# First layer's shift and scale loaded by halves of the features, with the query's first-half products between the halves

## The reference, cut to what matters

```
def modulation(silu_cond, w_mod_l, b_mod_l):
    m = silu_cond @ w_mod_l + b_mod_l
    return jnp.split(m[:, None, :], 6, axis=-1)      # sh1, sc1, g1, sh2, sc2, g2

def modulate(x, w, shift, scale):
    return rms_norm(x, w) * (1 + scale) + shift

sh1, sc1, g1, sh2, sc2, g2 = modulation(silu_cond, lw['w_mod'], lw['b_mod'])
out, ctx_tensors = token_mixer(modulate(x, lw['norm1'], sh1, sc1), lw, rope, ctx)
# in token_mixer: a_q, a_k, a_v, h_q, ... = split(h @ lw['w_in'])
```

## Time and profile before

| | us |
|---|---|
| median of 3 runs | 1380.81 (1379.59 to 1381.5) |
| profiled execution | 1384.76 |
| its span, first to last instruction | 1382.9 |
| PE busy in it | 1292.7 (93%) |
| DVE, ACT, POOL busy | 484.3, 315.1, 271.0 |
| mean granted clock of TensorE | 0.995 |

### The profile page before, as it was taken

How to read it: one execution, slowest core, us unless ns; L and a number is a source line. 1 busy time by engine, 2 the same in 40 slices (tenths; PEclk the granted TensorE clock), 3 DMA queues, 4 the chain that set the end, 5 groups by cost and what they waited for, 6 DMA issues and landing times.

```text
span 1382.9 us, 17520 instructions
## 1 busy us (share of the span) xinstructions
PE 1292.7 (93%) x6873; PEld 732.2 (53%) x6874; DVE 484.3 (35%) x896; ACT 315.1 (23%) x487; POOL 271.0 (20%) x231
## 2 busy tenths in 40 slices
PE   6999999999999898789999999999999998999877
PEld 2665545567555554345546554556755454555433
DVE  1324425865125401011144343388612541101112
ACT  2116624641001100000021563366100110000000
POOL 1640006841010100000028000486111010000001
PEclk9899999999999999999999999999999999999999
DMA  9799425762633999999984113377355299899997
GB/s 359 247 312 338 154 93 184 246 243 82 242 148 140 367 425 422 424 424 426 419 314 156 65 63 120 123 246 258 114 204 205 80 358 422 334 424 426 425 427 294
DMA packets 114586, 371.88 MB, mean 269 GB/s; under 512 B 17601, under 2 KB 32609, under 8 KB 97873
## 3 DMA queue, kind: packets, MB, share of 16 engines
q1 hardware_dynamic: 84320, 329.70, 61.2%
q0 software_dynamic: 6608, 21.96, 4.4%
q10 hardware_dynamic: 23584, 19.21, 4.1%
HBM read 341.42 MB, written 29.43 MB: 268 GB/s over the span
## 4 chain that ended last, share of the span: by engine, by line
PE 78%; DMA 11%; DVE 6%; issue 2%; ACT 1%; SPq 1%; ACTq 0%; DVEq 0%; POOL 0%
PE pG L1822 25%; PE pS L1924 12%; PE pG L1814 11%; PE pG L1942 6%; PE pG L2084 6%; DMA ring<-in_w_exp_down_dram 3%; PE pX L1726 3%; DMA ring<-in_w_exp_up_dram 3%; DMA rows_nw<-in_w_exp_gate_dram 3%; PE pX L1924 2%; PE pG L1759 2%; DMA ring<-in_w_mod_dram 2%; PE pS L1866 1%; PE pX L1904 1%; PE pX L1890 1%
## 5 line engine op out<-in xcount | busy, mean ns | idle before, releaser
L1822 PE MATMUL pG<-hT_gen,ring 128*128 128x384 f32 x1024 | 339.6, 489 | 1.6 <-ACT hT_gen L1103 1.6
L1822 PEld LDWEIGHTS pG<-hT_gen,ring 128*128 128x128 f32 x1024 | 191.8, 190 | 141.5 <-issue 13.7
L1924 PE MATMUL pS<-ring,hT_gen 128*64 128x256 f32 x1344 | 151.9, 380 | 13.5 <-DMA ring<-in_w_exp_up_dram 6.9
L1814 PE MATMUL pG<-ring,hT_gen 128*128 128x512 f32 (+1 forms) x384 | 149.8, 546 | 0.6 <-DVE hT_gen L1282 0.6
L1924 PEld LDWEIGHTS pS<-ring,hT_gen 128*64 128x64 f32 x1344 | 100.5, 137 | 67.2 <-issue 11.8
L1655 DVE TENSOR_TENSOR hT_gen<-pS,hT_gen 128x256 f32<-128x256 f32 x32 | 19.2, 601 | 315.9 <-PE pS L1924 315.9
L1814 PEld LDWEIGHTS pG<-ring,hT_gen 128*128 128x128 f32 x384 | 72.0, 191 | 70.0 <-issue 64.6
L863 POOL DMA_INDIRECT ring<-y_scr,idx x12 | 11.4, 952 | 459.5 <-ACTq L1181 456.4
L1942 PE MATMUL pG<-ring,brow 128*64 128x512 f32 x352 | 80.4, 598 | 11.1 <-DVE brow L1658 8.9
L2084 PE MATMUL pG<-ring,hT_gen 128*128 128x512 f32 x192 | 83.1, 592 | 0.0
L1135 ACT COPY hT_gen<-pG 128x512 f32<-128x512 f32 x30 | 17.6, 586 | 266.1 <-PE pG L1942 255.3
(11 more groups left out here) (325 smaller groups left out, 1614.2 us busy)
## 6 DMA issues: line engine op xcount, KB each, us to landing
ring<-in_w_mod_dram SPq DMA_DIRECT2D x24, 2048.0 KB, 8.3
ring<-in_w_exp_up_dram SPq DMA_DIRECT2D x22, 2048.0 KB, 27.4
ring<-in_w_in_dram SPq DMA_DIRECT2D x20, 2048.0 KB, 9.0
ring<-in_w_exp_down_dram SPq DMA_DIRECT2D x20, 2048.0 KB, 23.9
ring<-in_w_exp_gate_dram SPq DMA_DIRECT2D x20, 2048.0 KB, 24.2
modb<-in_w_exp_up_dram SPq DMA_DIRECT2D x10, 2048.0 KB, 27.1
hT_gen<-in_w_exp_down_dram SPq DMA_DIRECT2D x10, 2048.0 KB, 27.1
rows_nw<-in_w_exp_gate_dram SPq DMA_DIRECT2D x10, 2048.0 KB, 25.0
```

What stands on the lines that cost most here:

```text
L1814: ins = pe.matmul(ps[:, 0:width], hT[:, k, t * P:(t + 1) * P], w[:, k, 0:width], start=(k == 0), stop=(k == KC - 1))
L1822: ins = pe.matmul(ps[:, 0:TOK], w[:, k, c0:c0 + P], src[:, k, :], start=(k == 0), stop=(k == nk - 1))
L1924: ins = pe.matmul(dst[64 * hf:64 * hf + 64, 0:256], x[:, k, :], w[k][:, 256 * hf:256 * (hf + 1)], start=(k == 0), stop=(k == KC - 1))
```

## The change

The two pairs are formed anew: pair 0 is m = 0 and 2 (shift and scale of the first half of the features), pair 1 is m = 1 and 3. Each load of a pair becomes two DMAs of 1 MB, of 512 columns each. The query's weights leave the ring's order in the first layer and are loaded in two halves of 1 MB over the features (`q_half`, into `first_q`), one behind each pair. The wait of ACT ahead of the token rows is dropped. On PE all three tiles are transposed between the two halves of pair 0; then follow pair 0's column turns, the query's products over the first four chunks for tiles 0 and 1, pair 1, the same for tile 2, pair 1's column turns, and then the products over the last four chunks for all tiles, accumulated in banks 2, 4 and 6, which held the transposed first chunks. Of the idle products the two between the loads of pair 0 and the two behind it are gone; the three at the start stay. DVE applies scale and shift of the first chunks to all three tiles before pair 1's columns; ACT squares before it copies.

```diff
-COL_MODS = [0, 1, 2, 3, 12, 13, 14, 15]
+MOD_ORDER = [0, 2, 1, 3] + list(range(4, DEPTH * MODS))
+COL_MODS = [0, 2, 1, 3, 12, 13, 14, 15]
@@ mix_units
-    units = [("mod", m) for m in range(MOD_FIRST)] if L == 0 else []
-    for kind in ("q", "kv", "hq", "ff", "fb", "i", "g"):
+    units = [("mod", m) for m in MOD_ORDER[:MOD_FIRST]] if L == 0 else [("q", 0)]
+    for kind in ("kv", "hq", "ff", "fb", "i", "g"):
@@ groups
-    gs = [(k, 2 * j + i) for j in range(MOD_FIRST // 2) for k in ("mod", "mc") for i in range(2)] if L == 0 else []
-    for kind in ("q", "kv", "hq", "ff", "fb", "i", "g"):
+    gs = [(k, m) for j in range(2) for k in ("mod", "mc") for m in (j, j + 2)] if L == 0 else [("q", t) for t in range(NT)]
+    for kind in ("kv", "hq", "ff", "fb", "i", "g"):
@@ build
+        first_q = S[:, 3072:7168].rearrange("p (k n) -> p k n", k=KC)
@@ SP
             def mod_pair(j, hf):
-                c0 = 1024 * j
-                sp.dma_start(pair_of(j)[:, 4 * hf:4 * hf + 4, :],
-                             a["w_mod"][0].rearrange("(k p) n -> p k n", p=P)[:, 4 * hf:4 * hf + 4, c0:c0 + 1024]
-                             ).then_inc(landed[2 * j + hf], 16)
+                for i in range(2):
+                    c0 = 512 * j + 1024 * i
+                    sp.dma_start(pair_of(j)[:, 4 * hf:4 * hf + 4, 512 * i:512 * (i + 1)],
+                                 a["w_mod"][0].rearrange("(k p) n -> p k n", p=P)[:, 4 * hf:4 * hf + 4, c0:c0 + 512]
+                                 ).then_inc((landed[2 * j + hf], pair_in[2 * j + hf])[i], 16)
+
+            def q_half(hf):
+                sp.dma_start(first_q[:, 4 * hf:4 * hf + 4, :],
+                             a["w_in"][0].rearrange("(k p) n -> p k n", p=P)[:, 4 * hf:4 * hf + 4, 0:512]
+                             ).then_inc(first_q_in[hf], 16)
@@ SP, the loop over the units
                         mod_pair(n // 2, n % 2)
+                        if n % 2 == 1:
+                            q_half(n // 2)
@@ ACT
-            act.wait_ge(landed[0], 16)
             act.dma_start(xs[:, 0, :], a["x_prompt"][0]).then_inc(x_in, 16)
@@ ACT, first layer
-                    for m in range(2):
-                        mod_copy(L, m)
                     for t in range(NT):
                         norm1_square(L, t)
-                    for m in range(2, MOD_FIRST):
+                    for m in MOD_ORDER[:MOD_FIRST]:
                         mod_copy(L, m)
@@ DVE, first layer
-                    for m in range(2):
-                        mod_cols(m)
                     for t in range(NT):
                         norm1_mean(L, t)
                     for t in range(NT):
                         norm1_rows(L, t)
-                    mod_cols(2)
-                    dve.wait_ge(mc_evac, 3)
-                    norm1_out(L, 0)
-                    mod_cols(3)
-                    for t in range(1, NT):
+                    for m in MOD_ORDER[0:2]:
+                        mod_cols(m)
+                    dve.wait_ge(mc_evac, 2)
+                    for t in range(NT):
                         norm1_out(L, t)
+                    for m in MOD_ORDER[2:4]:
+                        mod_cols(m)
                     dve.wait_ge(small_in, SMALL_LOADS)
@@ DVE, query copies
-                    ps = sync_group(L, ("q" if isq else "kv", t))
+                    if isq and L == 0:
+                        dve.wait_ge(first_q_done, t + 1)
+                        ps = bank[2 + 2 * t]
+                    else:
+                        ps = sync_group(L, ("q" if isq else "kv", t))
@@ PE
+            def first_q_products(t, hf):
+
+                for k in range(4 * hf, 4 * hf + 4):
+                    ins = pe.matmul(bank[2 + 2 * t], hT[:, k, t * P:(t + 1) * P], first_q[:, k, :],
+                                    start=(k == 0), stop=(k == KC - 1))
+                return ins
@@ PE, first layer
                     idle_products(3, 7)
-                    mod_pair(0, lambda: idle_products(2, 7))
-                    idle_products(2, 7)
-                    mod_pair(1, lambda: norm_turn(2 * L, 0))
-                    for t in range(1, NT):
-                        norm_turn(2 * L, t)
+                    mod_pair(0, lambda: [norm_turn(0, t) for t in range(NT)])
+                    for m in MOD_ORDER[0:2]:
+                        mod_cols(0, m)
+                    pe.wait_ge(first_q_in[0], 16)
+                    for t in range(NT - 1):
+                        pe.wait_ge(hT_v, t + 1)
+                        first_q_products(t, 0)
+                    mod_pair(1, lambda: None)
+                    pe.wait_ge(hT_v, NT)
+                    first_q_products(NT - 1, 0)
+                    for m in MOD_ORDER[2:4]:
+                        mod_cols(0, m)
+                    pe.wait_ge(first_q_in[1], 16)
+                    for t in range(NT):
+                        pe.wait_ge(hT_a, t + 1)
+                        first_q_products(t, 1).then_inc(first_q_done, 1)
...
```

More of the change, by code:

```diff
@@ L336, in build @@
         landed = [sem(f"landed{s}") for s in range(9)]
+        first_q_in = [sem("first_q_in0"), sem("first_q_in1")]
+        first_q_done = sem("first_q_done")
+        pair_in = [sem(f"pair_in{i}") for i in range(4)]
         spare_in = sem("spare_in")
@@ L513, in build @@
         EVAC = {
-            "mod": lambda L, i: (mod_evac, i + 1),
+            "mod": lambda L, i: (mod_evac, MOD_ORDER.index(i) + 1),
             "mc": lambda L, i: (mc_evac, COL_MODS.index(i) + 1),
@@ L534, in mod_parts @@
         def mod_parts(m):
-            return modb[:, 2, 0, 512 * (m % 2):512 * (m % 2 + 1)]
+            b = MOD_ORDER.index(m) % 2
+            return modb[:, 2, 0, 512 * b:512 * (b + 1)]
         def rows_before(m, parity):
@@ L894, in mod_copy @@
                 ps = sync_group(L, ("mod", m))
-                if m - 2 in COL_MODS:
-                    act.wait_ge(group, gno(0, ("mc", m - 2)) + 1)
-                elif m >= 2:
+                pos = MOD_ORDER.index(m)
+                before = MOD_ORDER[pos - 2] if pos >= 2 else None
+                if before in COL_MODS:
+                    act.wait_ge(group, gno(0, ("mc", before)) + 1)
+                elif pos >= 2:
                     act.wait_ge(part_out[m % 2], 16 * rows_before(m, m % 2))
@@ L1773, in mod_pair @@
                     pe.wait_ge(landed[2 * j + hf], 16)
+                    pe.wait_ge(pair_in[2 * j + hf], 16)
                     for i in range(2):
-                        m = 2 * j + i
+                        m = j + 2 * i
                         if hf == 0:
@@ L1789, in mod_pair @@
                             finish_group(ins)
-                for i in range(2):
-                    mod_cols(0, 2 * j + i)
+            def first_q_products(t, hf):
[3 more added lines that the diff above has]
+                return ins
             def mods_behind(L, kind):
@@ L1801, in mod_cols @@
                 ps = start_group(L, ("mc", m))
-                pe.wait_ge(mod_evac, m + 1)
+                pe.wait_ge(mod_evac, MOD_ORDER.index(m) + 1)
                 for c in range(4):
@@ L1978, in _ @@
                     outputs_summed(L - 1, NT - 1, 1)
-                for t in range(NT):
+                for t in range(NT if L > 0 else 0):
                     pe.wait_ge(hT_v, NT * 2 * L + t + 1)
```

## The result

The changed kernel took 1386.35 us (median of 7 runs, 1385.1 to 1388.58) against 1381.5 us (7 runs, 1379.35 to 1385.61): 4.85 us slower, ratio 1.0035, 95% interval 1.0021 to 1.0050. Forecast was 1384.9, 4.1 slower than the median then known. A second series gave 1386.84, ratio 1.0042 (1.0029 to 1.0056).

A forecast was written before the change was run, and what follows sets the result against it. The start's chain, loads of w_mod and then an unbroken stream of query products on TensorE, was taken as the bound. Third query copy 67.9 plus 0.2 for POOL, 68.1 against 64.05: 4.1 slower, 1380.8 + 4.1 = 1384.9 us; range 1378.5 to 1389.5.

The forecast's parts named there:

- Token rows and their rate: Start, ACT's queue: issue at 8.0 instead of 11.39, two thirds of the bytes; squares at 18.3 instead of 23.48 us.
- Rival 2: Start: SP's row of loads holds up the token rows, squares at 23.5 or later, 5.2 us more, 1390.1; chance 0.12.
- The order on TensorE: Start: 8 us idle before the transposes at 22.6, these at half clock (5.4 us), first query product at 36.8 us.
- the two waits: TensorE waiting for DVE and ACT: 1.7 us before the first query product, 1.8 us before the second halves.
- The clock from the mod products on: TensorE after the transposes: still half clock, mod products 3.64 us and column turns 3.50 us.
- a slow start of the query products: First query products on TensorE: a first stretch at half clock, 1.7 us added.
- the fall behind the third hole: TensorE after the 1.8 us wait before the second halves: clock falls again, 0.9 us added (0 to 2.6).
- the mark: Start of the copy of the query's third tile: 64.05 us before, 67.9 forecast; shifts pass to the end one to one.
- POOL: POOL's work on the keys, ready at the mark plus 26.1 to 27.1 us: slack nearly gone, 0.2 us added (0 to 1).
- rival 4: A tie: half clock in the transposes, full from the mod products on, a fall behind thin work; 1381.6 us; chance 0.22.
- I carry the difference over to the median: Whole kernel: the profiled execution's 3.95 us above the median of 1380.81 was carried over, keeping 64.05 us as base.

The follow-up runs named there:

- with idle products: Changed kernel plus nine idle products in the 8.5 us TensorE gap ahead of the first transposes: 1384.66 us, ratio 1.0036 to the kernel before.
- pair 0 ahead: Changed kernel with the second half of pair 0 ahead of the three tiles' transposes: 1384.91 us, ratio 1.0022 to the kernel before.
- tile 2 behind: Changed kernel with tile 2's first-half query products behind pair 1's column turns: 1382.74 us, ratio 1.0010 to the kernel before.
- token rows late: Changed kernel with ACT's wait for the first w_mod load put back: 1388.62 us, ratio 1.0046 to the kernel before.

## Why the prediction was right, and where it was wrong

*Token rows and their rate: right to 0.7 us.* Squares at 18.88 and 19.04 in two profiles, where 18.3 was said; issue at 7.86. Over 12 to 17 us the two queues moved as many packets, twice the bytes for the token rows (packets, MB, share of 16 engines), as the earlier trace rows had led to expect:

```profile
q10 hardware_dynamic: 340, 1.33, 67.2%
q1 hardware_dynamic: 344, 0.67, 35.7%
```

The Trainium skill ("DMA: Bandwidth & Descriptors", Queues, rings and completion order) has each DMA engine go round-robin between its queues, a packet at a time; the even counts agree with it. Rival 2 did not come: ACT's two issues took 0.40 and 0.44 us, while SP's longest took 8.46 us (least/median/most ns of an issue, then from when to when they came):

```profile
L609 SPq DMA_DIRECT2D ring<-in_w_mod_dram x8: 397/790/8461, 3.1 to 20.1; - x8
```

*The order on TensorE: right.* A hole of 8.48 us (8 said), transposes at half clock in 5.38 (5.4), 1.75 and 1.94 for the two waits (1.7 and 1.8), a second fall at 52.6, worth 1.7.

*The clock from the mod products on: wrong.* Mod products and turns were put at 3.6 and 3.5 us, as in the earlier trace rows; they took 2.0 and 1.9, 3.2 us less, and of the 1.7 us of a slow start of the query products 0.2 came, 1.5 less. Against that the fall behind the third hole cost 1.7 us in full, where 0.9 was added for it, and the transposes began 0.4 us later than said; the other terms are off by some 0.2 us each at most. Together the mark is 3.3 us ahead of the 67.9 forecast for it, 3.4 with the 0.2 for POOL. The clock was back at 28.5 to 29.0, after 5.4 us of transposes without a pause. That is the mechanism of rival 4. Its sum gives a mark of 64.8, measured 64.67 and 64.94, so close in part by chance: it takes off the 1.7 and 1.6 us, but keeps the slow start, which did not come, and only 0.9 for the fall.

*"I carry the difference over to the median": wrong, 3.7 us or more.* This is the step that failed most. The profile of before had its clock down for 13.7 us, from the fall near 30.7 to 44.4; the mean clocks say that most of its runs have much less, and the one other profile has its mark at 60.38. That execution, 1382.24 us, is itself above the median: 1380.63 less the 1.9 us around the span and the 1318.8 to 1320.7 behind the mark puts a usual mark at 58.0 to 59.9 (an estimate). The prediction gave the execution's distance from the median (3.95 us) and took it for noise around it; it was in the start, in the very rows on which the sum was built. With 60.4 as base and 68.1 as forecast the answer would have been 7.7 us slower; with 64.8 as forecast and 64.05 as base 0.8 slower, next to no change. The two errors have opposite signs, and only so is 4.1 near the measured 4.85: the size was met by luck.

*Where the loss is.* Against the second profile of before the mark is 4.3 to 4.6 us later. From these profiles: the changed kernel spends 2.7 us of half clock on transposes and the first mod products (5.38 less 2.84, and 2.0 less 1.85) and 1.7 behind the third hole, 4.4 in all; the kernel before 1.5 (3.42 less 1.92). Clock makes 2.9 of it. The other 1.5 is what remains, and no run splits it off; I put it down to order: behind the landing of the last pair (34.2) only 12 products were left, but the chain that sets the mark no longer starts there.

*POOL: right.* The last key was done at 90.89 + 0.54, the key's transposes are in the group that begins at 91.19; no wait is seen, and the span less the mark is that of before.

```profile
90.89 0.54 POOL L817 TENSOR_SCALAR ring<-ring 128x128 f32<-128x128 f32 x1
...
91.19 1.04 PE L1742 MATMUL pX<-const,ring 128*128 128x128 f32 x8
```

What stays open: why the clock stayed down for 13.7 us in one execution of before and for 3.4 in another with the same work; why it fell behind the second hole, 1.75 us each time, in four versions (with idle products, pair 0 ahead, tile 2 behind, token rows late) and in neither profile of the changed kernel; and why the first of pair 0's products started at 12.18 in one profile of the changed loads and at 14.73 in another (tile 2 behind), as token rows and weights shared the engines.

## What to carry to other kernels

Before a sum is built on one profiled execution, compare its time and its mean clock with those of the other runs: 4 us above the median with a lower clock is a warning that the stretch you are reading may be the unusual one. The same holds for the profile of an experiment. Work that is moved ahead to fill a wait for a load must not be put behind something that arrives later than that load: here the mod products of half a pair stood behind the token rows. Starting them on their own landing, with the turns behind tile 0, ready products over the third hole and the first hole filled, turned 5 us lost into 5 us won; the first step alone gave less than half of the loss back. A TensorE that waits can cost twice, in the wait and in the half clock behind it; a swap that puts ready products over a 1.9 us wait took back more than the wait (ratio 1.0010 beside 1.0035 and 1.0042, some 3.5 to 4.4 us).

## What the runs showed of the hardware

- The same program was at 1.2 GHz for 13.7 and for 3.4 us at the same place in two executions, 3.7 us apart at the mark.
- Uninterrupted transposes of 5.4 us at 1.2 GHz ended with the clock back at 28.5 to 29.0 in the changed kernel; idle products through a hole of 8.5 us kept it up there, 24 transposes in 2.84 us instead of 5.38.
- A hole of 1.75 us, with 1.9 us of column turns ahead of it, had a fall of the clock behind it in four profiles of versions of the changed kernel (5.37 us instead of 3.67 for the next eight instructions) and none in the two of the changed kernel itself.
- With loads of 1 MB queued one behind another SP spent up to 8.46 us on the issue of one; ACT's issues beside it took 0.4, and its data flowed some 3 us after the issue.
